# A two-layer hybrid backbone on one core: the post and pre norms in two token groups

## What is computed

```python
hx = rmsnorm(x, g_pre1) * (1.0 + sc1) + sh1       # hc: the same of e, with the context's vectors
ux = hx @ w_in                                    # q, k, v, pool, conv and three gate inputs
yx = mixer_out(q, k_all, v_all, u_pool, u_conv, u_gate, lp)   # ends in merged @ w_out
x = x + gt1 * rmsnorm(yx, g_post1)
hx2 = rmsnorm(x, g_pre2) * (1.0 + sc2) + sh2
x = x + gt2 * rmsnorm(swiglu(hx2, w_ffn_in, w_ffn_out), g_post2)
```

## Time and profile before

| | |
|---|---|
| runs | 2355.81, 2353.72, 2355.42 us |
| profiled execution | 2353.74 us; its span 2351.9 us |
| TensorE's mean granted clock | 0.951 of full |
| TensorE (PE) busy | 2138.1 us, 91% |
| VectorE (DVE) busy | 1374.1 us, 58% |
| GpSimd (POOL) busy | 822.3 us, 35% |
| ScalarE (ACT) busy | 737.9 us, 31% |
| chain that ended last | TensorE 66%, VectorE 26%, ScalarE 3% |

### The profile page before, as it was taken

How to read it: one execution, slowest core, us unless ns; L and a number is a source line. 1 busy time by engine, 2 the same in 40 slices (tenths; PEclk the granted TensorE clock), 3 DMA queues, 4 the chain that set the end, 5 groups by cost and what they waited for, 6 DMA issues and landing times.

```text
span 2351.9 us, 27666 instructions
## 1 busy us (share of the span) xinstructions
PE 2138.1 (91%) x11298; PEld 1825.3 (78%) x11298; DVE 1374.1 (58%) x1707; ACT 737.9 (31%) x1055; POOL 822.3 (35%) x336
## 2 busy tenths in 40 slices
PE   6889999889999699999999968897869997999997
PEld 6777787678888588888888856676658885888885
DVE  6459899953588557846516554889974414101114
ACT  2447511133323322222112233661224333222222
POOL 3220134243443333222322332103545644444442
...
GB/s 281 37 45 1 19 54 54 31 69 50 121 139 161 81 126 117 175 113 133 100 80 132 84 81 54 28 2 71 64 57 81 99 109 80 99 99 91 99 90 70
DMA packets 62910, 204.44 MB, mean 87 GB/s; under 512 B 7104, under 2 KB 8256, under 8 KB 62528
## 3 DMA queue, kind: packets, MB, share of 16 engines
...
## 4 chain that ended last, share of the span: by engine, by line
PE 66%; DVE 26%; ACT 3%; issue 3%; POOL 1%; DMA 1%; ACTq 0%; DVEq 0%
PE ps L443 57%; DVE conv_acc L1299 12%; PE ps L461 3%; DVE unit_stats L1260 2%; DVE pt0l L1280 1%; DVE pt1l L1280 1%; DVE probs L1274 1%; DVE norm_tmp L1120 1%; PE ps L492 1%; PE ps L512 1%; PE ps L614 1%; DVE ps L1162 1%; PE ps L473 1%; DVE x L1129 1%; PE ps L483 1%
## 5 line engine op out<-in xcount | busy, mean ns | idle before, releaser
L374 POOL TENSOR_TENSOR w_l<-w_raw,w_h 128x1024 fp32r<-128x1024 f32 x296 | 756.9, 2560 | 1383.4 <-ACT w_h L748 1383.3
L443 PE MATMUL ps<-h_h,w_h 128*128 128x512 f32 (+1 forms) x1968 | 601.3, 360 | 25.2 <-ACT t L940 18.9
L443 PE MATMUL ps<-h_l,w_h 128*128 128x512 f32 (+1 forms) x1968 | 595.0, 357 | 0.0
L443 PE MATMUL ps<-h_h,w_l 128*128 128x512 f32 (+1 forms) x1968 | 593.8, 356 | 0.0
L443 PEld LDWEIGHTS ps<-h_h,w_h 128*128 128x128 f32 x1968 | 373.6, 190 | 86.4 <-ACT t L940 20.2
L443 PEld LDWEIGHTS ps<-h_l,w_h 128*128 128x128 f32 x1968 | 373.9, 190 | 54.9 <-issue 1.2
L443 PEld LDWEIGHTS ps<-h_h,w_l 128*128 128x128 f32 x1968 | 373.4, 190 | 55.1
L748 ACT ACTIVATE w_h<-w_raw 128x1024 fp32r<-128x1024 f32 (+2 forms) x296 | 281.1, 951 | 243.3 <-PE ps L443 188.2
L1299 DVE SCALAR_TENSOR_TENSOR conv_acc<-conv_in,vec,conv_acc 128x783 f32<-128x783 f32 (+1 forms) x240 | 290.0, 1256 | 2.8
L1162 DVE CUSTOM_DVE_ANT_0 ps<-ada_raw,c_row 128x1024 f32<-128x1024 f32 x160 | 284.2, 1776 | 9.8 <-DMA ada_raw<-in_ada 4.8
L443 PE MATMUL ps<-mid_l,w_h 128*128 128x512 f32 (+1 forms) x528 | 157.8, 353 | 0.0
(11 more groups left out here) (178 smaller groups left out, 2856.3 us busy)
## 6 DMA issues: line engine op xcount, KB each, us to landing
...
```

What stands on the lines that cost most here:

```text
L374: nc.gpsimd.tensor_tensor(wl[:, s % RING, :], raw[:, s % RAW, :], wh[:, s % RING, :], ALU.subtract).then_inc(split, 1)
L443: ins = nc.tensor.matmul(at(out, c0, c1), w[:, s % RING, b * P:(b + 1) * P], m[:, kt, c0:c1], start=(kt == 0 and n == 0), stop=(kt == n_k ...
```

## The change

The last four of the eight slabs of w_out, and of the last group of FFN-out, are done in two token groups a and b (`token_halves`: 384 columns each in layer 0, 256 in layer 1; group a of layer 0 is the context and 128 latent tokens). `skewed` does four slabs for a, then the same four for b, with the sums of a between them; both halves of a slab have banks of their own. The sums become one fp32 product of a 128x128 matrix of ones with the squares (`post_stat`, `pre_stat`), which leaves the sum on every partition in bank 6 or 7, R(h). ScalarE takes its root in place (`wide_root`, with the scaling), VectorE its reciprocal in place (`inverse`, L1274). Residual, squares, normalising and halves run for a, with y tiles of b put between, and then for b. Old x is read back from memory into the room of h_l (x_in). The first two FFN tiles, and in layer 1 k, v, q0 and q1, run for a and then for b. Behind them layer 1's `finish` of a tile stands two gemms later than the tile; finish(q3) stands behind cval in both layers. S_KV is two full slabs where it was four halves; stores of x stand elsewhere. GROUPS is (8, 6, 8).

```diff
-GROUPS = (8, 8, 6)
+GROUPS = (8, 6, 8)
...
+SKEW = KT - RING
...
-                    load(2, 4)
-                    load(3, 4)
+                    load(2, KT)
+                    load(3, KT)
...
+        def token_halves(lo):
+            return [(lo, (lo + T) // 2), ((lo + T) // 2, T)]
...
+            def boundary(ly, st, lo, src, reload, nxt, at):
+                (a0, a1), (b0, b1) = token_halves(lo)
+                residual(ly, st, 0, a0, a1, src, reload, nxt, {2: at, 5: at + 1})
+                lows(*nxt, 0, a0, a1)
+                split_run(at + 2, at + RING)
+                residual(ly, st, 1, b0, b1, src, reload, nxt, {})
+                lows(*nxt, 1, b0, b1)
...
+            def post_stat(ly, st, h, c0, c1):
+                def run():
+                    pe.wait_ge(*seen("ysum", ly, st, h))
+                    nc.tensor.matmul(R(h, c0, c1), ones, t3[:, c0:c1], start=True,
+                                     stop=True).then_inc(*pe_done.up("stat", ly, st, h))
+                return run
+            def pre_stat(ly, st, h, c0, c1):
+                def run():
+                    pe.wait_ge(*seen("sq2", ly, st, KT - 2, h))
+                    for k in range(0, KT, 2):
+                        ins = nc.tensor.matmul(R(h, c0, c1), ones, square(k)[:, c0:c1], start=(k == 0),
+                                               stop=(k == KT - 2))
+                    ins.then_inc(*pe_done.up("stat", ly, st, h))
+                return run
+            def skewed(ly, st, nxt, first, nb, xh, xl, freed):
+                (a0, a1), (b0, b1) = token_halves(lo_of(ly))
+                for j in range(SKEW, KT):
+                    if j % 2 == 0:
+                        pe.wait_ge(*seen("free", *freed, j // 2))
+                    gemm([(bank[j - SKEW][:, 0:a1 - a0], a0, a1)], [(first + j, nb)], xh, xl,
+                         last=False).then_inc(*pe_done.up("half", ly, st, j))
+                for j in range(SKEW, KT):
+                    n = (j - SKEW + 2) % 4
+                    hooks = {}
+                    if j == SKEW:
+                        hooks = {4: post_stat(ly, st, 0, a0, a1)}
+                    elif j == KT - 1 and nxt:
+                        hooks = {1: pre_stat(*nxt, 0, a0, a1)}
+                    pe.wait_ge(*seen("free", "half", ly, st, SKEW + n, 0))
+                    gemm([(bank[n][:, 0:b1 - b0], b0, b1)], [(first + j, nb)], xh, xl, hooks=hooks)
...
-                for n, name in enumerate(tiles):
-                    w = n % 2
-                    take(w, "gemm", ly, name)
-                    if name == "v":
-                        s = s0 + S_KV
-                        gemm_pair(A, [(s, s + 1, 4), (s + 2, s + 3, 4)], pre_ready, full)
-                    elif name != "k":
-                        gemm(A[w], [(s0 + S_Q + n - 2, 8)], hh, hl, cols)
-                    if n:
-                        finish(tiles[n - 1])
+                if ly == 0:
+                    spread(0, "pre1", 0, "pre1")
+                    gemm_pair([into(A[0], full), into(A[1], full)], (s0, s0 + 1),
+                              lambda k: seen("hl", 0, "pre1", k, 0))
+                    last_use[0], last_use[1] = ("gemm", 0, "k"), ("gemm", 0, "v")
+                    finish("k")
+                    for n in range(2):
+                        take(n, "gemm", 0, f"q{n}")
+                        gemm(into(A[n], cols), [(s0 + S_Q + n, 8)], hh, hl)
+                        finish(("v", "q0")[n])
+                else:
+                    (a0, a1), (b0, b1) = token_halves(0)
+                    def early(name, c0, c1):
+                        return [(tile_cols(1, name, c0, c1), c0, c1)]
+                    gemm_pair([early("k", a0, a1), early("v", a0, a1)], (s0, s0 + 1),
+                              lambda k: seen("hl", 1, "pre1", k, 0), last=False,
+                              hooks={4: post_stat(0, "post2", 1, b0, b1)})
+                    for n in range(2):
+                        gemm(early(f"q{n}", CTX, a1), [(s0 + S_Q + n, 8)], hh, hl, last=False)
+                    pre_stat(1, "pre1", 1, b0, b1)()
+                    gemm_pair([early("k", b0, b1), early("v", b0, b1)], (s0, s0 + 1),
+                              lambda k: seen("hl", 1, "pre1", k, 1))
+                    last_use[0], last_use[1], last_use["B"] = (("gemm", 1, "k"), ("gemm", 1, "v"),
+                                                               ("gemm", 1, "q1"))
+                    last_use["OD"] = ("wide", 1, "pre1", 1)
+                    for n in range(2):
+                        gemm(early(f"q{n}", b0, b1), [(s0 + S_Q + n, 8)], hh, hl)
+                        finish(("k", "v")[n])
+                for n in range(2, 4):
+                    take(n % 2, "gemm", ly, f"q{n}")
+                    gemm(into(A[n % 2], cols), [(s0 + S_Q + n, 8)], hh, hl)
+                    finish(tiles[n + 1 if ly == 0 else n])
                 take(0, "cgate", ly, 0)
-                gemm(A[0], [(s0 + S_CONV, 8)], hh, hl, cols)
-                finish(tiles[-1])
+                gemm(into(A[0], cols), [(s0 + S_CONV, 8)], hh, hl)
+                if ly:
+                    finish("q2")
                 take(1, "cval", ly, 0)
-                gemm(A[1], [(s0 + S_CONV + 1, 8)], hh, hl, cols)
+                gemm(into(A[1], cols), [(s0 + S_CONV + 1, 8)], hh, hl)
+                finish("q3")
...
-                for j in range(KT):
+                for j in range(SKEW):
                     take(j % 2, "out", ly, j)
-                    gemm(A[j % 2], [(s0 + S_OUT + j, 8)], mh, ml, cols,
+                    gemm(into(A[j % 2], cols), [(s0 + S_OUT + j, 8)], mh, ml,
                          k_ready=(lambda k: seen("ml", ly, k)) if j == 0 else None)
-                pe.wait_ge(*seen("ysum", ly, "post1"))
-                token_sums(t3, lo, "post1").then_inc(*pe_done.up("stat", ly, "post1"))
-                spread(lo, "post1", ly, "post1")
-                for k in range(0, KT, 2):
-                    square_sum(ly, "pre2", lo, k)
-                spread(lo, "pre2", ly, "pre2")
-                f0 = 0
+                skewed(ly, "post1", (ly, "pre2"), s0 + S_OUT, KT, mh, ml, ("out", ly))
+                def wide(f, h, c0, c1):
+                    return [[(bank[n][:, 0:c1 - c0], c0, c1)] for n in FF_BANKS[f, h]]
+                (a0, a1), (b0, b1) = token_halves(lo)
+                f0, s = 0, s0 + FF_IN[0]
+                for j, f in ((4, 0), (5, 0)):
+                    pe.wait_ge(*seen("free", "half", ly, "post1", j, 1))
+                gemm_pair(wide(0, 0, a0, a1), (s, s + 1), lambda k: seen("hl", ly, "pre2", k, 0), last=False,
+                          hooks={4: post_stat(ly, "post1", 1, b0, b1)}).then_inc(*pe_done.up("ffh", ly, 0, 0))
+                for j in (6, 7):
+                    pe.wait_ge(*seen("free", "half", ly, "post1", j, 1))
+                gemm_pair(wide(1, 0, a0, a1), (s + 2, s + 3), None, last=False,
+                          hooks={6: pre_stat(ly, "pre2", 1, b0, b1)}).then_inc(*pe_done.up("ffh", ly, 1, 0))
+                gemm_pair(wide(0, 1, b0, b1), (s, s + 1), lambda k: seen("hl", ly, "pre2", k, 1))
+                gemm_pair(wide(1, 1, b0, b1), (s + 2, s + 3), None)
+                last_use[0], last_use[1] = ("ffb", ly, 1, 0), ("ffb", ly, 0, 0)
                 for g, nf in enumerate(GROUPS):
                     for f in range(f0, f0 + nf):
+                        if f < 2:
+                            continue
                         s = s0 + FF_IN[g] + 2 * (f - f0)
-                        if f == 0:
-                            take(0, "ffa", ly, f)
-                            take(1, "ffb", ly, f)
-                            gemm_pair(A, [(s, s + 1, 8)], lambda k: seen("hl", ly, "pre2", k), cols)
-                            continue
                         take(0, "ffa", ly, f)
-                        gemm(A[0], [(s, 8)], hh, hl, cols)
+                        gemm(into(A[0], cols), [(s, 8)], hh, hl)
                         take(1, "ffb", ly, f)
-                        gemm(A[1], [(s + 1, 8)], hh, hl, cols)
+                        gemm(into(A[1], cols), [(s + 1, 8)], hh, hl)
                     s = s0 + FF_OUT[g]
-                    for j in range(KT):
...
+            def wide_root(ly, st, h, c0, c1):
+                act.wait_ge(*seen("stat", ly, st, h))
+                nc.scalar.activation(R(h, c0, c1), R(h, c0, c1), ACT.Sqrt, scale=1.0 / D,
+                                     bias=eps[:, 0:1]).then_inc(*act_tmp.up("rs", ly, st, h))
...
+            def boundary(ly, st, lo, y_half, nxt, shift, at):
+                (a0, a1), (b0, b1) = token_halves(lo)
+                def squares(h, c0, c1, ks):
+                    for k in ks:
+                        square_x(*nxt, h, c0, c1, k, *seen("x", ly, st, k, h))
+                for j in range(SKEW, KT):
+                    y_half(j, 0, a0, a1)
+                wide_root(ly, st, 0, a0, a1)
+                rounds(at)
```

(44 more changed lines are left out.)

460 lines of the change are left out of this document (266 added, 194 removed).

## The result

The changed kernel takes 2383.32 us (median of 4 runs, 2380.57 to 2386.54) beside 2355.61 for the kernel before: 1.0106 times as long, 95% interval 1.0081 to 1.0131 (the two medians by themselves give 1.0118, inside that interval). It is slower, by 28 us by the medians and 25 by the ratio. Run once more beside the last experiment it was 1.0096 (1.0066 to 1.0127), with a median of 2385.2 us. The kernel before came at 2352 to 2358 us or at 2362 to 2369 in the runs beside the experiments, while its four runs here all lie in the lower cluster, so a few us of any comparison between ratios are the reference's own. The profiled execution took 2386.54 us, its span 2384.7, so 32.8 more than the span of the earlier trace rows.

What follows compares the result with a forecast made beforehand. The prediction took TensorE as the bound, 91% busy, with 139 us lost at four norm boundaries. Terms -8 - 2.3 - 1.5 + 3.4 + 18.5 + 8.4 = +18.5 on 2353.74 gave 2372, stated as 2373; range 2340 to 2388.

Steps and rivals of the forecast that it cites:

- Tiles of layer 1: Layer 1, k and v to scores: later finishes leave rotations and copies bare ahead of cgate and cval; loss 18.5 us.
- Tiles of layer 0: Layer 0 ahead of the scores: q3's head sums and rotation behind cval lie bare, a 10.8 us stop; loss 8.4 us.
- The wide reciprocal: VectorE's reciprocal in the norms, over 384 or 256 columns instead of 6: 2.55 or 1.75 us each.
- The rival that it streams: Wide reciprocals at 1.04 ns a column, 2 us less in 14 places: -3 us, 2352; chance 0.12.
- First boundary: Layer 0, w_out through post norm, residual and pre norm to the FFN's second pair: 102 against 110.0, gain 8 us.
- VectorE free at 61.5: First boundary: VectorE free for group b's chain 61.5 us after the fifth slab starts; that chain ends at 75.6.
- Second boundary: Layer 0's FFN to layer 1's k/v: TensorE waits some 10 us for b's squares; k/v end 96.5 against 93.1, loss 3.4.
- Third boundary and end: Layer 1's w_out to its FFN gains 2.3 us (74.7 against 77.0); the kernel's end gains 1.5 (39.9 against 41.4).
- Eight cold restarts: TensorE stops lower the granted clock, 2 us charged per restart; some 16 us of the forecast time.
- the clock holds: Rival: TensorE's granted clock stays up through the stops; +3 us, 2358; chance 0.16.
- eightfold reciprocal: Rival: each wide reciprocal takes 8 x 1.04 ns a column; +31 us, 2386; chance 0.06.
- A wait unseen: Rival: an unforeseen wait, such as a weight ring starving while GpSimd does norms; over 2388 us; chance 0.05.

Runs made afterwards that it cites:

- the last experiment: Kernel with undelayed finishes and pre sums issued as squares come, plus unread filler products on TensorE in its stops: 2335.77 us, 0.9885.
- the experiment that undoes it: Changed kernel with every tile's finish one gemm behind its tile again, in both layers: 2352.73 us, 0.9969.
- The experiment with sums as they come: Kernel with every finish one gemm behind its tile, plus each pre-sum product issued as its squares come, not all four after the last: 2334.66 us, 0.9888.
- The filler: Changed kernel plus unread fp32 products of constants on TensorE at ten places with stops: 2376.0 us, 1.0065.

## Why the prediction was right, and where a term was off

The sign and the range (2340 to 2388) held; the forecast of 2373 was 10 us low. In the traces it is +32.7 us where the sum was +18.5. By its steps:

- **Tiles of layer 1, +18.5.** Measured 18.6 in the trace, and 17.8 in the trace of the experiment that undoes it (19 by the ratios). v's transposes came 21.6 us behind k and v (21.4), the stops ahead of cgate and cval were 6.2 (6.4).
- **Tiles of layer 0, +8.4.** The stop is 10.62 (10.8). The trace has 9.8; the 1.4 us more are the first pair and the slower pace of the tiles' gemms, and the second profile of the same kernel has 8.4.
- **The wide reciprocal.** 2.563 and 1.764 us against 2.55 and 1.75. Nearly all of their 24 us came back when they were taken out. By the Trainium skill ("VectorE: DVE Perf Modes", "First, the fixed hardware budget") the reciprocal iterates with a repeat count of 8. That it costs eight plain passes, 8 times 1.04 ns a column and 3.35 us a piece, was my estimate from it and not the page's; the trace has 6.2 ns a column, six times as long as a plain instruction's 1.04. The rival that it streams says "half of them bare", but its sum of -3 takes off 21 us, nearly all of them, and all of them are on the chain.
- **First boundary, gain 8.** 2.8 us. This is the term that was mis-sized, and at two steps of it, both of group b; the steps of group a, up to 64.8, held within 1.4 us. One is "VectorE free at 61.5": it is free at 64.5, because two low halves of a take 4 us longer beside GpSimd's splits, and b's squares come 2.7 us late. Rows 5 had such a case, an add of 768 columns at 2.41 us where others take 0.96, counted in as ordinary work. The other is "Pre products and the last tile make it 79.4", with the four products at the pace of an engine that has just worked, 2.8 us. They stand behind a stop of 5.09 us, had 0.55 of the clock, and took 5.11, 2.3 us more. The experiment with sums as they come shows what the products in one piece cost: 17.5 us over the boundaries in the traces.
- **Second boundary, loss 3.4.** 4.9; k and v end at 98.1 instead of 96.5, and group b's four products took 5.07 us here too.
- **"At nothing: the order 8, 6, 8 (the same tiles)."** Nearly: it costs a stop of 1.25 us for VectorE in the FFN of layer 0. The rest of the 4.9 us there is a slower pace of TensorE at full clock, which no term held and which two other kernels with this order don't have.
- **Third boundary and end, gain 3.8.** 6.1.
- **Eight cold restarts, 16 us.** The filler took back 7 to 10, with some of the stops left 2 to 3 us open. Neither confirmed nor refuted as a sum.
- **Scores to w_out in layer 0** has 3.2 us that I have no cause for. In the other profiles that have the same code there it is 0.6 to 3.3.

As for the rivals, "the clock holds" fell by the windows, the streaming and the eightfold reciprocal by 2.563 us. "A wait unseen" was there, not as a starved ring of weights: 1.25 us for VectorE's add, and VectorE's own 4 us beside the splits of GpSimd at each of two boundaries. None of these was foreseen; with the clock of b's products and the slower pace they are most of what the forecast lacks, and the range, which reached 15 us above it, was wide enough for them.

The change thus holds a gain and three losses. In token groups the boundaries gain: the kernel with groups, undelayed finishes and stepwise sums has 0.9888, the one with the same sums and no groups 1.0045, some 37 us apart; the two differ in the order of slabs and the reload of x as well. The wide sums cost 11 us where they were measured alone, without groups; inside the groups the one other form that was tried was no better. The order of the finishes took 32 by the ratios (28 in the traces), and pre sums issued in one piece 19. The version with the last two mended is the best of this study, 26 us faster than the kernel before and some 50 faster than the changed one.
